# RWKV scan: block inverses from 16- and 32-wide products of non-zero blocks, and a later place for VectorE's second running sum

## The chip, the core and the metric

One core of a Trainium2 chip runs the whole program in one launch. The metric is the device time of one execution in microseconds. The engines are TensorE (PE, with its weight loads as PEld), VectorE (DVE), ScalarE (ACT), GpSimd (POOL) and SyncE (SP), which here only issues DMAs.

## The reference

Two layers of a diffusion transformer at batch 1, 512 tokens of 1024 with a context of 256. Layer 0 mixes by neighbourhood attention and a Hyena convolution, layer 1 by an RWKV-7 scan in both directions; each is followed by a SwiGLU network. The change lies in the scan of layer 1, whose step is

```python
def update(s, w_t, k_t, v_t, kk_t, a_t):
    sa = jnp.einsum('ebhvk,ebhk->ebhv', s, kk_t)
    return s * w_t[..., None, :] - sa[..., :, None] * (kk_t * a_t)[..., None, :] + v_t[..., :, None] * k_t[..., None, :]
```

over 256 + 512 tokens, 16 heads of 64, directions e = 0 and e = 1 (the second reversed), with a readout of the 512.

## The kernel before, in words

The scan is done in chunks of 64 tokens, 12 chunks per head and direction. Within a chunk the steps couple through a strictly triangular 64x64 matrix A, so the kernel needs the inverse of (1 + A) for 12 chunks x 2 directions x 2 heads. A tile of 128 partitions holds two heads' channels; the scan walks over the eight such tiles (`CT` = 8). Chunks are laid out as (p, j): p = 0, 1 is the half of the partitions, j = 0 to 5; h is the head.

The loop `ROUNDS` (line 2031) is a software pipeline written out by hand: in one round, tile i is solved and scanned, tile n = i + 1 is prepared (decays, Gram matrices), tile c = i + 2 has its keys normalised. Every engine has its own copy of the loop, `scan_pe` (2193), `scan_act` (2539), `scan_dve` (2667), `scan_pool` (2153) and `scan_sp` (2057). `Marks` (1968) numbers the finished operations of each engine, and waits are on these numbers, so the tables `PEM`, `DV`, `AC` and `PO` (1985 to 2005) are the order of work. TensorE's products go to PSUM banks in turns, two banks for each name of `BACK` and `FRONT`.

The inverse of tile i is made in this way.

- Masked A (`mask_gram`, `mA_0`, `mA_1`) of tile n comes from the Gram products `A_0`, `A_1` (L2259). SyncE writes its 16x16 diagonal blocks to DRAM with eight DMAs (L2106) and reads them back with one (L2109), one block to a partition of `BLK`.
- GpSimd inverts them in fifteen elimination steps (L2179, L2180: `sub`) and transposes them (`turn`, L2188). SyncE writes both forms to DRAM (L2131), and eight DMAs (L2137) put them on the diagonal of `XY`, which GpSimd has cleared (L2166). `XY` holds for e = 0, 1 the inverse X (a = e) and its transpose Y (a = 2 + e), 64x64 for each (h, j), zero outside the blocks. `xy_in` counts these DMAs.
- In the next round TensorE doubles the blocks twice (`squares`, L2245): 24 products of 64x64 each for `w16_e` = A X, masked by VectorE to the blocks just off the diagonal (`level`, L2688); `x16_e`, `y16_e` = the products of Y and X with it, taken off X and Y (`lessen`, L2692); then `w32_e` and `y32_e` in the same way for blocks of 32. That is 10 x 24 = 240 products and ten VectorE operations of 768 elements per partition.
- The finished Y is the left side of the solves `oo_0`, `oo_1`, `oo_2` (L2307), evicted by ScalarE (L2581). Then come the transition `mr` (L2319), states, outputs and the chain over the chunks (L2385, VectorE L2784).

Between these stand tile n's LoRA product `l01`, `l11` (L2228), tile i-1's transpose `vr` (L2418), and on VectorE tile n's running sums of the log decay (`sums`, L2698, one for each direction), `kin` (L2704), `ba` (L2709), `bt` (L2713), which `A_0` and `A_1` need.

Of the kernel before, what the change touches and what calls it, by code (L numbers as in the profile page):

```python
# [40 lines left out]
def shape_constants():  # L41
# [33 lines left out]
    lev = []  # L75
    for m in (16, 32):
        same = (s // (2 * m)) == (q // (2 * m))
        later = same & (s % (2 * m) >= m) & (q % (2 * m) < m)
        lev.append([later, later.T])
    lev = np.array(lev).astype(f4)  # L80
    t["levelmask"] = np.ascontiguousarray(np.tile(lev.transpose(2, 0, 1, 3), (2, 1, 1, 1)))
# [7 lines left out]
def hybrid_dit_kernel(nc, a, out):  # L89
# [3 lines left out]
    with ctx:  # L93
# [1775 lines left out]
        def mixes_dve(v):  # L1869
# [44 lines left out]
        TOKK, KINT, BVT, XY, OO, MT, NE = carve(ARENA[3], [2 * T, 2 * T, 2 * T, 4 * T, 4 * T, 2 * T, 2 * T])  # L1914
        KROOT, VROOT, KA1, W2S, A2S, BLK, YB, PROD, XB, LV, RSTEP, G2S, G2S2 = carve(
            ARENA[5], [2 * NCH // 2, L // TC, CT, 128, 128, 512, 512, 512, 512, 4 * TC, 2 * L, 128, 128])
# [8 lines left out]
        WI = OO[:, 0:2 * T]  # L1925
        OO = OO.rearrange("p (e h j o t) -> p e h j o t", e=2, h=2, j=6, o=2)
        KM, WI, KINT, BVT = (x.rearrange("p (e h j t) -> p e h j t", e=2, h=2, j=6) for x in (KM, WI, KINT, BVT))
# [7 lines left out]
        LV = LV.rearrange("p (l d t) -> p l d t", l=2, d=2)  # L1935
# [32 lines left out]
        class Marks(dict):  # L1968
# [36 lines left out]
        PO = Marks(pool_done, ((1, "s00 s10 s01 s11 sub turn"),))  # L2005
# [10 lines left out]
        BACK = "w16_0 w16_1 x16_0 y16_0 x16_1 y16_1 w32_0 w32_1 y32_0 y32_1 oo_0 oo_1 oo_2 mr_0 mr_1 mr_2 n_0 yt n_1".split()  # L2016
# [136 lines left out]
        def scan_pool(pool):  # L2153
            sub = Chain(pool, sub_step)
            for _, n, _ in ROUNDS:
# [975 lines left out]
```

## Time and profile before

| | us |
|---|---|
| median of 3 runs | 2502.8 |
| lowest, highest | 2498.32, 2507.42 |
| profiled execution, its own time | 2497.23 |
| its span | 2495.4 |
| TensorE, VectorE, ScalarE, GpSimd busy | 2289.3, 947.5, 655.8, 863.6 |

The span runs from the first to the last instruction on the engines; the execution's time adds what lies around it. In the timeline a group of like instructions is one row, with the time from the first start to the last end, the number of records, and in brackets how long the engine was idle before it and what ended that ("issue": it waited for nothing that the profile shows). An f32 matmul of the program makes two matmul records and two weight-load records on TensorE; an order listing, below, counts it once. The scan's eight rounds with a tile i run from 1541 to 2022 us.

### The profile page before, as it was taken

What the parts mean: (1) busy time and instruction counts of PE and PEld (TensorE: products, weight loads), DVE (VectorE), ACT (ScalarE), POOL (GpSimd) and SP (SyncE); (2) the same over time, 40 slices, a digit from 0 to 9 for tenths busy, and PEclk for the clock granted to TensorE, in tenths of its full rate; (3) what the DMA queues carried; (4) which work ended last, traced back from release to release, by engine and by line L of the source; (5) the groups of instructions that cost most, each with busy time, mean ns of one, the idle gap of its engine ahead of it and who ended that gap; (6) DMA issues with size and microseconds to landing.
All of it is one profiled execution on the core that took longest, in us unless ns stands there. A gap on an engine that the chain in (4) does not pass through costs nothing. (4 is left out here: it accounts for less than half of the span.)

```text
span 2495.4 us, 50322 instructions
## 1 busy us (share of the span) xinstructions
PE 2289.3 (92%) x22240; PEld 1919.4 (77%) x22240; DVE 947.5 (38%) x1499; ACT 655.8 (26%) x1019; POOL 863.6 (35%) x699
## 2 busy tenths in 40 slices
PE   5999989979699999999969998999999987999997
PEld 3778855655399999999828987888888765888785
DVE  3112265980410000122397125676777524000123
ACT  4111066421410000122232133444444223011112
POOL 2222300100133434434215453333333243666562
PEclk9999999989799999999979999999999988999998
DMA  6555530001012121111212342222222121222221
GB/s 255 207 210 187 211 111 18 1 34 42 26 60 67 59 65 61 59 67 60 53 59 67 108 158 56 43 42 43 43 43 41 23 96 66 92 92 93 92 94 66
DMA packets 139265, 204.05 MB, mean 82 GB/s; under 512 B 87783, under 2 KB 97511, under 8 KB 131912
## 3 DMA queue, kind: packets, MB, share of 16 engines
q1 hardware_dynamic: 139080, 201.26, 25.0%
q8 instruction: 155, 2.54, 0.4%
q14 instruction: 30, 0.25, 0.0%
HBM read 183.93 MB, written 17.30 MB: 81 GB/s over the span
## 5 line engine op out<-in xcount | busy, mean ns | idle before, releaser
L258 POOL CAST TMP_r<-WR 128x1024 fp32r<-128x1024 f32 x120 | 126.8, 1056 | 728.2 <-DMA WR<-in_ffn_w_dram 438.4
L277 PE MATMUL PS<-H_r,TMP_r 128*128 128x384 f32 (+1 forms) x1088 | 330.2, 359 | 10.9 <-DVE Y_r L494 10.9
L277 PE MATMUL PS<-Y_r,TMP_r 128*128 128x384 f32 (+1 forms) x1088 | 330.0, 358 | 3.7 <-DVE H_r L494 3.7
L260 POOL TENSOR_TENSOR WR_r<-WR,TMP_r 128x1024 fp32r<-128x1024 f32 x120 | 289.5, 2412 | 9.6
L417 DVE TENSOR_TENSOR P<-TMP,PS 128x768 f32 (+1 forms) x44 | 36.1, 821 | 562.9 <-PE PS L277 562.9
L277 PEld LDWEIGHTS PS<-H_r,TMP_r 128*128 128x128 f32 x1088 | 202.2, 190 | 27.4 <-DVE Y_r L494 11.6
L277 PEld LDWEIGHTS PS<-Y_r,TMP_r 128*128 128x128 f32 x1088 | 201.5, 190 | 19.3 <-DVE H_r L494 4.0
L277 PE MATMUL PS<-H_r,WR_r 128*128 128x384 f32 x736 | 191.4, 341 | 0.0
L400 ACT ACTIVATE TMP<-PS 128x768 f32<-128x768 f32 (+1 forms) x44 | 31.0, 706 | 526.5 <-PE PS L277 526.5
L594 PE MATMUL PS<-H_r,TMP_r 128*128 128x384 f32 x704 | 150.8, 336 | 3.2 <-DVE H_r L632 2.2
L277 PE MATMUL PS<-Y_r,WR_r 128*128 128x512 f32 x352 | 139.4, 396 | 0.0
L277 PEld LDWEIGHTS PS<-H_r,WR_r 128*128 128x128 f32 x736 | 133.4, 189 | 0.0
L594 PEld LDWEIGHTS PS<-H_r,TMP_r 128*128 128x128 f32 x704 | 124.5, 188 | 3.8 <-DVE P L417 2.5
L1750 PE MATMUL PS<-P_r,TMP_r 128*128 128x384 f32 (+1 forms) x448 | 114.4, 348 | 5.9 <-POOL WR_r L2149 4.3
L594 PE MATMUL PS<-Y_r,TMP_r 128*128 128x512 f32 x352 | 109.7, 393 | 2.2 <-DVE Y_r L632 2.2
L270 POOL TENSOR_TENSOR WR_r<-WR,TMP_r 128x1024 fp32r<-128x1024 f32 x44 | 107.2, 2437 | 3.5
L1633 PE MATMUL PS<-H_r,TMP_r 128*128 128x384 f32 x352 | 94.7, 351 | 7.6 <-POOL WR_r L260 7.4
L268 POOL CAST TMP_r<-WR 128x1024 fp32r<-128x1024 f32 x44 | 46.7, 1061 | 153.7 <-DMA WR<-in_down_dram 153.7
L2147 POOL CAST TMP_r<-WR 128x1024 fp32r<-128x1024 f32 x24 | 42.6, 1776 | 144.2 <-DMA WR<-in_rw_w_rkv_dram 144.2
L1633 PE MATMUL PS<-H_r,WR_r 128*128 128x384 f32 x352 | 92.3, 344 | 0.0
L632 DVE TENSOR_TENSOR H_r<-P,H_r 128x768 fp32r<-128x768 f32 x44 | 44.2, 1042 | 124.2 <-ACT H_r L625 124.2
L1750 PE MATMUL PS<-P_r,WR_r 128*128 128x384 f32 (+1 forms) x320 | 91.3, 350 | 0.0
(320 smaller groups left out, 4538.3 us busy)
## 6 DMA issues: line engine op xcount, KB each, us to landing
WR<-in_ffn_w_dram SPq DMA_DIRECT2D x88, 512.0 KB, 3.5
TMP<-in_mod_w_dram SPq DMA_DIRECT2D x40, 1024.0 KB, 4.9
WR<-in_down_dram SPq DMA_DIRECT2D x44, 512.0 KB, 3.5
WR<-in_mix_w_in_dram SPq DMA_DIRECT2D x24, 512.0 KB, 7.0
WR<-in_rw_w_rkv_dram SPq DMA_DIRECT2D x24, 512.0 KB, 4.2
P<-in_mod_w_dram SPq DMA_DIRECT2D x4, 2048.0 KB, 21.7
vkr_dram<-extra SPq DMA_DIRECT2D x16, 384.0 KB, 4.8
scan_front<-vkr_dram SPq DMA_DIRECT2D x16, 384.0 KB, 4.0
```

The costliest lines, as they stand in the source:

```text
L258: nc.gpsimd.tensor_copy(hi, raw).then_inc(weights_hi, 1)
L260: nc.gpsimd.tensor_tensor(lo, raw, hi.bitcast(F32), ALU.subtract).then_inc(weights_split, 1)
L268: nc.gpsimd.tensor_copy(hi, raw).then_inc(weights_hi, 1)
L270: nc.gpsimd.tensor_tensor(lo, raw, hi.bitcast(F32), ALU.subtract).then_inc(weights_split, 1)
L277: last = nc.tensor.matmul(PS[:, bank + b, 0:h1 - h0], w, x[:, h0:h1], start=k + p == 0, stop=k == CT - 1 and p == 2)
L400: nc.scalar.activation(as_halves(GATE[:, u, 0:d.n], d.n), halves(bank, d.n), ACT.Silu)\
L417: nc.vector.tensor_tensor(as_halves(dst, d.n), as_halves(GATE[:, u, 0:d.n], d.n), halves(4 * u + 2, d.n), ALU.mult).then_inc(d.unit_free, 1)
L594: last = nc.tensor.matmul(PS[:, bank, 0:h1 - h0], w[:, at:at + 128], x[:, q % 4, h0:h1], start=k + p == 0, stop=k == FT - 1 and p == 2)
L632: nc.vector.tensor_tensor(d.lo[:, q % 4, :], P[:, q % FT, 0:d.n], d.hi[:, q % 4, :].bitcast(F32), ALU.subtract).then_inc(hid_split, 1)
L1633: last = nc.tensor.matmul(PS[:, 2 * u + b, 0:HALF], w, x[:, HALF * b:HALF * b + HALF], start=k + p == 0, stop=k == CT - 1 and p == 2)
L1750: last = nc.tensor.matmul(PS[:, kept_bank(t) + b, 0:h1 - h0], wt, x[:, k, h0:h1], start=k + p == 0, stop=k == CT - 1 and p == 2)
L2147: nc.gpsimd.tensor_copy(hi, raw).then_inc(weights_hi, 1)
```

## The change

The two levels of doubling no longer multiply whole 64x64 matrices.

- `XY` holds pairs of 16-blocks, 32 columns instead of 64 (the DMAs put block b at column 16 (b mod 2)); it has half its size. `W16`, `W32` and `YF` are new tiles, `WI` and the level masks go, and a table `EDGE` of four columns takes the masks' place.
- First level: `w16` is 96 products (32 rows, 32 columns of A, 16 moving columns), on four row quarters in turn. One VectorE operation masks both directions into `W16`. `xy16` is 2 x 96 such products into two banks, and two VectorE operations take them off X and Y.
- Second level: `w32` is 48 products of 32x32, which VectorE negates into `W32`; `y32` is 96, half with `W32`, half with the identity, which brings the later block beside the earlier; VectorE copies one half of each direction's answer to `YF` (`yf_0`, `yf_1`).
- The other part of `YF`, the diagonal blocks, is made by GpSimd from `XY` (`yd_0`, `yd_1`, after `y16`), ahead of clearing `XY`; the clearing now waits for `y32` and not for `oo_2`.
- The solves read `YF`. `oo_0` and `oo_1` follow each other, and `oo_2` stands before `A_1`.
- On VectorE `sums(n, 1)` moves from between the answers of the first level to behind them and `f1`.

Per round this makes 96 + 192 + 48 + 96 = 432 products in place of 240.

On TensorE, one round from its first level to the transition, in the order of before (`TMP` and `scan_small` are the LoRA operands; `x48` counts matmuls of the program):

```order
L2245 MATMUL PS<-scan_back,scan_tokens 64x64 x48
L2245 MATMUL PS<-scan_back 64x64 x48
L2228 MATMUL PS<-TMP,scan_small 128x384 x4
L2245 MATMUL PS<-scan_back 64x64 x48
L2418 MATMUL PS<-ident,extra 128x128 x4
L2245 MATMUL PS<-scan_back,scan_tokens 64x64 x48
L2245 MATMUL PS<-scan_back 64x64 x48
L2307 MATMUL PS<-scan_back 64x128 x16
L2259 MATMUL PS<-scan_tokens,scan_front 64x64 x24
```

The same stretch after the change, where lines 2448 and 2450 alternate 96 times in all:

```order
L2408 MATMUL PS<-scan_back,scan_tokens 32x16 x96
L2246 MATMUL PS<-TMP,scan_small 128x384 x4
L2421 MATMUL PS<-scan_small,scan_back 32x16 x96
L2421 MATMUL PS<-scan_back,scan_small 32x16 x96
L2467 MATMUL PS<-ident,extra 128x128 x4
L2434 MATMUL PS<-scan_back,scan_tokens 32x32 x48
L2448 MATMUL PS<-scan_back,scan_small 32x32
L2450 MATMUL PS<-scan_back,scan_front 32x32
```

Behind it follow L2316 (`oo_0`, `oo_1`) x32, one Gram x24, L2316 (`oo_2`) x16 and the other Gram. Every inverse product has moved from the 64x64 form to 32-wide forms, and there are more of them.

On VectorE, the same round before, from the first level's answer to the second's (L2698 is the running sum, L2803 `f1`):

```order
L2688 TENSOR_TENSOR scan_back<-PS,scan_small 128x768 x2
L2698 SCALAR_TENSOR_TENSOR scan_front<-extra,scan_front 128x768
L2692 TENSOR_TENSOR scan_back<-scan_back,PS 128x768 x2
L2698 SCALAR_TENSOR_TENSOR scan_front<-extra,scan_front 128x768
L2692 TENSOR_TENSOR scan_back<-scan_back,PS 128x768 x2
L2803 SCALAR_TENSOR_TENSOR extra<-extra,PC,PS 128x512
```

and after the change:

```order
L2732 TENSOR_TENSOR scan_small<-PS,scan_small 128x2x12x16
L2759 SCALAR_TENSOR_TENSOR scan_front<-extra,scan_front 128x768
L2737 TENSOR_TENSOR scan_back<-scan_back,PS 128x2x12x16 x2
L2857 SCALAR_TENSOR_TENSOR extra<-extra,PC,PS 128x512
L2759 SCALAR_TENSOR_TENSOR scan_front<-extra,scan_front 128x768
L2748 TENSOR_SCALAR scan_small<-PS 128x384
L2765 TENSOR_TENSOR scan_tokens<-scan_front 128x12x63
```

The second running sum now stands behind both answers and `f1`, and before the second level's answer (L2748).

The diff, cut to its core:

```diff
-        TOKK, KINT, BVT, XY, OO, MT, NE = carve(ARENA[3], [2 * T, 2 * T, 2 * T, 4 * T, 4 * T, 2 * T, 2 * T])
+        TOKK, KINT, BVT, XY, YF, OO, MT, NE = carve(ARENA[3], [2 * T, 2 * T, 2 * T, 2 * T, 2 * T, 4 * T, 2 * T, 2 * T])
...
-            (0, "w16_0 w16_1 x16_0 y16_0"), (1, "l01 l11"), (0, "x16_1 y16_1"), (-1, "vr"),
-            (0, "w32_0 w32_1 y32_0 y32_1 oo_0"), (1, "A_0"), (0, "oo_1"), (1, "A_1"),
-            (0, "oo_2 mr_0 mr_1"), (1, "kT_0"), (0, "mr_2 n_0 cg yt"), (1, "kT_1"), (0, "n_1"), (1, "tV"),
+            (0, "w16"), (1, "l01 l11"), (0, "xy16"), (-1, "vr"),
+            (0, "w32 y32 oo_0 oo_1"), (1, "A_0"), (0, "oo_2"), (1, "A_1"),
+            (0, "mr_0 mr_1"), (1, "kT_0"), (0, "mr_2 n_0 cg yt"), (1, "kT_1"), (0, "n_1"), (1, "tV"),
...
-        PO = Marks(pool_done, ((1, "s00 s10 s01 s11 sub turn"),))
+        PO = Marks(pool_done, ((1, "s00 s10 s01 s11"), (0, "yd_0 yd_1"), (1, "sub turn")))
...
-                            sp.dma_start(XY[at:at + BK, :, :, :, BK * b:BK * b + BK].rearrange("s a h j t -> s (a h j) t"),
+                            col0 = BK * (b % 2)
+                            sp.dma_start(XY[at:at + BK, :, :, :, col0:col0 + BK].rearrange("s a h j t -> s (a h j) t"),
...
                 if n:
-                    pool.wait_ge(pe_done, PEM["oo_2", n - 1])
+                    pool.wait_ge(dve_done, DV["y16", n - 1])
+                    for e in range(2):
+                        PO.done(nc.gpsimd.tensor_scalar(YF[:, e, :, :, 32 * e:32 * e + 32], XY[:, 2 + e], EDGE[:, 2 + e:3 + e],
+                                                        None, ALU.mult), f"yd_{e}", n - 1)
+                    pool.wait_ge(pe_done, PEM["y32", n - 1])
+                    pool.wait_ge(pool_done, PO["yd_1", n - 1])
                     sub.link(nc.gpsimd.memset(XY[:, :, :, :, :].rearrange("p a h j t -> p (a h j t)"), 0.0))
...
+            def first_level(i):
+                b = back("w16", i)
+                pe.wait_ge(xy_in, 128 * i + 128)
...
+                out = sixteen(b)
+                for e in range(2):
+                    for h, j in ALL_HJ:
+                        for g, r in enumerate(Q4):
+                            c = 32 * (g % 2)
+                            last = nc.tensor.matmul(out[r, e, h, j, :], AM[r, i % 2, e, h, j, c:c + 32],
+                                                    XY[r, e, h, j, EARLIER[e]], start=True, stop=True)
+                PEM.done(last, "w16", i)
+
+            def first_inverse(i):
...
+                    out = sixteen(bank)
+                    for e in range(2):
+                        for h, j in ALL_HJ:
+                            for r in Q4:
+                                last = nc.tensor.matmul(out[r, e, h, j, :], left(r, e, h, j), right(r, e, h, j),
+                                                        start=True, stop=True)
+                PEM.done(last, "xy16", i)
+
+            def second_level(i):
...
+                            last = nc.tensor.matmul(out[late, h, j, :], AM[early, i % 2, e, h, j, c:c + 32],
+                                                    XY[early, e, h, j, :], start=True, stop=True)
+                PEM.done(last, "w32", i)
+
+            def second_inverse(i):
...
+                            nc.tensor.matmul(out[early, h, j, :], W32[late, h, j, :], XY[late, 2 + e, h, j, :],
+                                             start=True, stop=True)
+                            last = nc.tensor.matmul(out[late, h, j, :], IDENT2[late, c:c + 32], XY[late, 2 + e, h, j, :],
+                                                    start=True, stop=True)
+                PEM.done(last, "y32", i)
...
                 if here(i):
-                    lessen(i, "x16_0", XY[:, 0])
-                    lessen(i, "y16_0", XY[:, 2])
-                if here(n):
-                    sums(n, 1)
-                if here(i):
-                    lessen(i, "x16_1", XY[:, 1])
-                    lessen(i, "y16_1", XY[:, 3])
+                    first_inverse(i)
...
                 if here(n):
+                    sums(n, 1)
+                if here(i):
+                    second_level(i)
+                if here(n):
                     after("kmul", n)
                     keys(n, 0)
                 if here(i):
-                    level(i, 1, 0)
-                    level(i, 1, 1)
+                    second_inverse(i, 0)
+                    second_inverse(i, 1)
                 if here(n):
                     based(n, 0)
```

## Rows read from the trace of the kernel before

**Rows 1.** The page: span, and the DMA queue (kind: packets, MB, share).

```profile
span 2495.4 us, 50322 instructions
...
q8 instruction: 155, 2.54, 0.4%
```

**Rows 2.** Windows (us; each engine: busy, records; PEclk, DMA share, GB/s), one round.

```profile
1848.70:1908.90 60.20, 57.48 (x1584) 49.62 (x1584) 44.39 (x73) 27.66 (x40) 21.62 (x38) 1.00 0.22 44
```

**Rows 3.** Timeline of TensorE (start, us, line, xcount, idle before), three rounds.

```profile
1726.50 4.47 PE L2245 MATMUL PS<-scan_back,scan_tokens 64*64 64x64 f32 x96 [2.24 <-DMA scan_back<-inv_dram]
1730.70 3.17 PE L2245 MATMUL PS<-scan_back 64*64 64x64 f32 x96
...
1848.70 3.01 PE L2245 MATMUL PS<-scan_back,scan_tokens 64*64 64x64 f32 x96 [0.45 <-DMA scan_back<-inv_dram]
1851.52 2.99 PE L2245 MATMUL PS<-scan_back 64*64 64x64 f32 x96
...
1865.42 1.80 PE L2307 MATMUL PS<-scan_back 64*64 64x128 f32 x29
...
1869.72 0.93 PE L2259 MATMUL PS<-scan_tokens,scan_front 64*64 64x64 f32 x48
...
1968.45 3.02 PE L2245 MATMUL PS<-scan_back,scan_tokens 64*64 64x64 f32 x96 [0.95 <-DMA scan_back<-inv_dram]
...
1983.23 5.29 PE L2307 MATMUL PS<-scan_back 64*64 64x128 f32 x93
```

**Rows 4.** Timeline of SyncE's queue and GpSimd, 1811 to 1848.

```profile
1811.27 4.43 SPq L2106 DMA_DIRECT2D blk_dram<-scan_tokens  x8
...
1840.03 5.81 SPq L2137 DMA_DIRECT2D scan_back<-inv_dram  x8
...
1819.80 0.23 POOL L2179 TENSOR_TENSOR scan_small<-scan_small 96x30 f32<-96x30 f32 x1 [4.32 <-DMA scan_small<-blk_dram]
```

**Rows 5.** Timeline of weight loads with "issue", and windows between them.

```profile
1938.00 0.13 PEld L2342 LDWEIGHTS PS<-scan_tokens,scan_back 64*64 64x64 f32 x2 [0.49 <-issue]
...
1945.94 0.21 PEld L2345 LDWEIGHTS PS<-scan_back,scan_tokens 64*64 64x64 f32 x8 [0.16 <-issue]
...
1957.60 0.21 PEld L2286 LDWEIGHTS PS<-scan_tokens,scan_front 64*64 64x64 f32 x8 [0.26 <-issue]
...
1937.99:1945.91 7.92, 7.91 (x254) 5.48 (x255) 5.35 (x8) 2.03 (x4) 4.53 (x10) 1.00 0.15 39
1945.92:1957.58 11.66, 10.52 (x255) 8.86 (x254) 8.52 (x25) 4.06 (x5) 9.77 (x21) 1.00 0.05 15
```

**Rows 6.** Timeline of TensorE and windows around the longest such stall.

```profile
1998.72 0.30 PE L2342 MATMUL PS<-scan_tokens,scan_back 64*64 64x64 f32 x8
...
1999.19 0.30 PE L2342 MATMUL PS<-scan_tokens,scan_back 64*64 64x64 f32 x8
...
2000.45 0.28 PE L2345 MATMUL PS<-scan_back,scan_tokens 64*64 64x64 f32 x4 [0.93 <-issue]
...
1998.10:1998.20 0.10, 0.10 (x21) 0.10 (x17) 0.00 (x0) 0.00 (x0) 0.00 (x0) 1.00 0.68 164
...
2001.60:2001.70 0.10, 0.00 (x0) 0.00 (x0) 0.10 (x1) 0.10 (x1) 0.00 (x0) 1.00 0.84 164
```

**Rows 7.** Timeline of VectorE and GpSimd: operations of 768, 512 elements, running sum.

```profile
1858.29 1.79 DVE L2692 TENSOR_TENSOR scan_back<-scan_back,PS 128x768 f32<-128x768 f32 x2
...
1710.63 0.68 DVE L2749 TENSOR_TENSOR scan_tokens<-PS,extra 128x512 f32<-128x512 f32 x1
...
1856.62 1.75 DVE L2698 TENSOR_TENSOR_SCAN scan_front<-extra,scan_front 128x768 f32<-128x768 f32 x1
...
1727.77 1.63 POOL L2161 TENSOR_SCALAR scan_front<-scan_front 128x768 f32<-128x768 f32 x2 [14.55 <-ACT scan_front L2543]
```

**Rows 8.** Windows with the granted clock: first level of a round, chain of the last.

```profile
1728.00:1731.00 3.00, 3.00 (x62) 3.00 (x61) 0.96 (x1) 0.47 (x1) 1.40 (x2) 0.50 0.00 0
...
2005.00:2006.00 1.00, 0.83 (x12) 0.65 (x13) 0.58 (x3) 0.30 (x1) 0.00 (x0) 0.50 0.00 0
```

More of the change, by code:

```diff
@@ L73, in shape_constants @@
     t["grammask"] = np.tile(gram, (2, 1, 1, 1)).astype(f4)
[L75 to L81, printed above, removed]
+    edges = np.stack([i % 32 >= 16, i % 32 < 16, i % 64 < 32, i % 64 >= 32], 1)
+    t["edges"] = edges.astype(f4)
     run = np.ones((128, T), f4)
@@ L2238, in tokens @@
                 PEM.done(last, name, n)
-            def squares(b, lhs, rhs):
-                for j in range(6):
-                    for h in range(2):
-                        for p, pr in enumerate(H2):
-                            last = nc.tensor.matmul(PS[pr, b + h, 64 * j:64 * j + 64], lhs(pr, h, j), rhs(pr, h, j),
-                                                    start=True, stop=True)
-                return last
             def turned(n, e):
@@ new lines, in first_inverse @@
+            def first_inverse(i):
+                b = back("xy16", i)
+                pe.wait_ge(dve_done, DV["w16", i])
+                for bank, left, right in ((b, lambda r, e, h, j: XY[r, 2 + e, h, j, :], lambda r, e, h, j: W16[r, e, h, j, EARLIER[e]]),
+                                          (b + 1, lambda r, e, h, j: W16[r, e, h, j, :], lambda r, e, h, j: XY[r, 2 + e, h, j, LATER[e]])):
+                    out = sixteen(bank)
+                    for e in range(2):
+                        for h, j in ALL_HJ:
[3 more added lines that the diff above has]
+                PEM.done(last, "xy16", i)
@@ new lines, in second_level @@
+            def second_level(i):
+                b = back("w32", i)
+                pe.wait_ge(dve_done, DV["x16", i])
+                out = thirty_two(b)
+                for h, j in ALL_HJ:
+                    for e in range(2):
+                        for p in range(2):
+                            early, late = Q4[2 * p + e], Q4[2 * p + 1 - e]
+                            c = 32 * (1 - e)
+                            last = nc.tensor.matmul(out[late, h, j, :], AM[early, i % 2, e, h, j, c:c + 32],
+                                                    XY[early, e, h, j, :], start=True, stop=True)
+                PEM.done(last, "w32", i)
@@ new lines, in second_inverse @@
+            def second_inverse(i):
+                b = back("y32", i)
+                pe.wait_ge(dve_done, DV["y16", i])
+                pe.wait_ge(dve_done, DV["w32", i])
+                for e in range(2):
+                    out = thirty_two(b + e)
+                    for h, j in ALL_HJ:
+                        for p in range(2):
+                            early, late = Q4[2 * p + e], Q4[2 * p + 1 - e]
+                            c = 32 * (1 - e)
+                            nc.tensor.matmul(out[early, h, j, :], W32[late, h, j, :], XY[late, 2 + e, h, j, :],
[3 more added lines that the diff above has]
+                PEM.done(last, "y32", i)
@@ L2411, in scan_pe @@
                 if here(i):
-                    level("x16", 1, "w16", Ym, Wm)
-                    level("y16", 1, "w16", Wm, Ym)
+                    first_inverse(i)
                 if here(i - 1):
@@ L2420, in scan_pe @@
                 if here(i):
-                    for e in range(2):
-                        level("w32", e, "x16", Am, Xm)
-                    for e in range(2):
-                        level("y32", e, "w32", Wm, Ym)
-                    pe.wait_ge(dve_done, DV["y32_0", i])
+                    second_level(i)
+                    second_inverse(i)
+                    pe.wait_ge(pool_done, PO["yd_1", i])
+                    pe.wait_ge(dve_done, DV["yf_0", i])
                     pe.wait_ge(act_done, AC["bv_1", i])
                     solve(i, "oo_0", [(0, j) for j in range(4)])
+                    pe.wait_ge(dve_done, DV["yf_1", i])
+                    solve(i, "oo_1", [(1, j) for j in range(4)])
                 if here(n):
@@ L2432, in scan_pe @@
                 if here(i):
-                    pe.wait_ge(dve_done, DV["y32_1", i])
-                    solve(i, "oo_1", [(1, j) for j in range(4)])
+                    solve(i, "oo_2", [(e, j) for e in range(2) for j in (4, 5)])
                 if here(n):
@@ L2441, in scan_pe @@
                 if here(i):
-                    solve(i, "oo_2", [(e, j) for e in range(2) for j in (4, 5)])
                     transition(i, 0)
@@ L2788, in scan_dve @@
                 if here(i):
-                    level(i, 0, 0)
-                    level(i, 0, 1)
+                    first_level(i)
                 if here(n):
```

88 lines of the change are left out of this document (48 added, 40 removed), and 4 rows, old and new, of the table DV.

## The prediction

> **What bounds the kernel now.** The page comes first: the profiled execution spans 2495.4 us [rows 1]. The change touches only the scan, so the next view is busy time by stretch. Seven of the eight iterations of the scan take about 60 us each; in the one I use, 1848.7 to 1908.9, TensorE is busy 57.5 of 60.2 us with 1584 matmul records, and as many weight-load records [rows 2]. Each f32 matmul of the program is two of each, so it costs four records.
>
> The timeline of TensorE then gives the stretch that the change rewrites [rows 3]. The first level starts at 1848.70, the first solve (L2307) at 1865.42: 16.7 us. The second Gram (L2259) starts at 1869.72 and takes 0.93 us, of which the end overlaps what follows, some 0.75 net; so the masked A is due 21.8 us after the start, give or take VectorE's mask, which follows both before and after. In the last iteration the stretch is 1968.45 to 1983.23, 14.8 us [rows 3].
>
> What releases the next first level is not TensorE's own work. It is the loop over memory: the masked A is sent out at 1811.27, comes back, GpSimd starts its fifteen steps at 1819.80, SyncE reads the results into XY from 1840.03 with eight DMAs, and TensorE starts at 1848.70 after 0.45 us of waiting for them [rows 3, 4]. From mask to start that is 37.4 us, and it does not get shorter. In the other iterations shown TensorE waited 2.24 and 0.95 us for the same DMA [rows 3]. So the two loops are nearly level, and **the time from the start of the first level to the second masked A counts one for one**, seven times; the eighth time the stretch up to the first solve counts.
>
> **The limit that decides.** TensorE's program is not at hand; it comes in pieces. The page has a DMA queue "instruction" with 155 transfers, 2.54 MB in all, 16.4 KB each [rows 1]. Three stalls of weight loads that the trace puts down to "issue", at 1938.00, 1945.94 and 1957.60, lie 254 + 255 and 255 + 254 records apart [rows 5]: with the few waits that aren't counted, 256 records, one piece. How long a piece takes is seen at the longest stall. A transfer starts in 1998.1 to 1998.2, TensorE's records stop, and resume at 2000.45 after 0.93 us; the next transfer starts in 2001.6 to 2001.7 [rows 6]. So a piece can be used 2.35 us after its transfer starts, and the next transfer starts 1.15 us after that: **3.5 us per 256 records, 13.7 ns per record, while only one piece is on its way**. Today's small products run two side by side, 96 matmul records in 2.82 us [rows 3], 14.7 ns per record with the loads counted: just slower than the supply, which is therefore unseen. Four side by side run 32 in 0.47 us, 7.3 ns per record [rows 6], which outruns it; such stretches are short now.
>
> **The change, part by part.** Per iteration the products of the two levels go from 240 matmuls of 64x64 to 96 + 192 + 48 + 96 = 432 of 32x16 and 32x32.
> - TensorE's own work. Now 480 pairs of records at 29.4 ns, 14.1 us. Afterwards 864 pairs. No row has 32x32 products. From above, the 14.7 ns of four 64x64 products side by side [rows 6] give 12.7 us; from below, half of it, 6.4 us, since half the columns are loaded. I take the lower, because the streamed columns shrink by as much or more. By itself that is a gain of 7.7 us.
> - Supply. 432 x 4 = 1728 records, and 24 of the LoRA product (four f32 matmuls) and the four transposes (two records each) in between, are 1752, or 6.8 pieces. At the start the rest of one piece and the next one are there; five or six are fetched within the stretch, 17.5 to 20.9 us, and with what runs before the first and after the last of them the first solve starts 20.0 to 22.5 us after the first level. I take the middle, 21.3 us, against 16.7. An iteration has 3168 records and a few waits, twelve pieces and a half, so both cases alternate.
> - VectorE. Ten operations of 768 elements, 1.79 us for two, become six of 384; one of 512 takes 0.68 [rows 7], so I take 0.5. It saves about 6 us per iteration of an engine that isn't the limit. The second running sum (1.75 us) [rows 7] now stands before the second level's answer. It ends before the supply brings the 96 matmuls' successors, so I cost it at nothing; were the supply no limit, the second level would wait for it some 2 us.
> - GpSimd. Two products of 384 elements (0.8 us, by half of the 1.63 that L2161's two of 768 took) [rows 7] wait for y16 and stand ahead of the clearing of XY; the clearing halves. GpSimd then waits for the blocks from memory for 4.32 us [rows 4], which hides both. The eight DMAs into XY have the same pieces and rows: nothing.
> - Order. The third solve moves ahead of the second Gram. Three solves of 1.75 us (the last iteration's three in a row took 5.29 [rows 3]) and two Grams of 0.75 lie between first solve and masked A, 6.75 us instead of 5.05. What TensorE saves behind it only lengthens its wait for XY.
>
> So without the clock the masked A is due at 21.3 + 6.75 = 28.1 us against 21.8: 6.3 us later, seven times, and 6.5 us in the last iteration: 50.6 us.
> - Clock. After a wait of 2.24 us the granted clock was 0.50, that is 1.2 GHz, in 1728 to 1731, 62 matmul records in 3 us instead of 34 per us [rows 3, 8]; and in the last iteration, where short bursts alternate with waits, it stood at 0.50 in 2005 to 2006 [rows 8]. With the supply as limit TensorE works in bursts of about a third of the time. I expect 1.2 GHz there, which the supply hides, and a start of the solves at that clock. One such stretch cost 1.4 us (96 records in 4.20 us instead of 2.82) [rows 3]; I take something under two, 2.5 us, eight times: 20 us.
>
> Sum: 50.6 + 20 = 70.6 us. The profiled execution took 2497.2 us, so 2567.8. It lies 5.6 us under the median of the runs shown, so I write 2570. Ends: five pieces everywhere and no loss of clock give (20.0 + 6.75 - 21.8) x 7 + 5.2 = 40 us, 2537; six pieces and 3.5 us of clock give 10.95 x 7 + 11.2 = 88, 2585.
>
> **Rivals.**
> 1. *Faster: the supply keeps up.* Then the stretch is 1.5 us for w16, 1.5 for the LoRA, 3.0 for the next 192 matmuls, 1.1 to x16, y16, f1 and the running sum 2.8 more, 0.5 for w32, 1.7 for y32, 0.6 to the first yf: 12.7 us. The masked A comes at 19.5, 2.3 us earlier; seven times, with 4 us in the last iteration, 20 us: 2477. It needs pieces that arrive in less than the 1 us that 128 pairs at 7.4 ns run; the break-even lies where five and a half pieces take 13 us, near 9 ns per record. Against it stand the stalls [rows 5, 6]. The Trainium skill (Runtime: NRT & Kernel Launch, section Instruction fetch mechanics) says that crossing a 16 KiB boundary is mostly hidden; by it this case would hold, and the trace's 0.93 us at such a boundary speaks against. Chance 0.10.
> 2. *Supply as the limit, clock kept:* 2497.2 + 50.6 = 2548. For it: a burst of small products may count as steady work. Chance 0.20.
> 3. *The clock stays down up to the second masked A:* the 6.75 us double, 7 x (6.3 + 6.75) + 12 = 103, 2601. Chance 0.08.
> 4. *Small products don't overlap:* they run at today's 29.4 ns whatever their size; 864 x 29.4 = 25.4 us with LoRA, transposes and handovers about 30 before the first solve, 13.3 us more, and 1.7 for the order: 7 x 15.0 + 13.3 = 118, 2616. The 32 in 0.47 us [rows 6] speak against it. The Trainium skill (TensorEngine Tiling, section Instruction Overhead) says that a small matmul costs as much as one of 60 columns, and that no factor should come from a dimension that is already small; by that the own work is an estimate of 12 to 14 us and the supply still decides. Chance 0.05.
>
> That the stretch lies beside something else and nothing shows: 0.02, since both loops contain it.
>
> **How the numbers follow.** The forecast has 0.55, rivals 2, 3 and 4 0.33: all slower, 0.88. Faster 0.10, same 0.02; 0.3%, 7.5 us, is what a measurement of this kernel can tell from no change. The range, 2535 to 2605, takes in both ends of the forecast, rival 2 and rival 3; it leaves out rival 4 and the faster case, and what a lasting low clock with six pieces would add.
>
> **What would show it.** Right: first solve 20 to 22.5 us after the first level; "issue" stalls every 256 records in it; about 24 transfers more in the instruction queue (1536 matmuls x 4 / 256); the period of an iteration near 69 us, mask to start still 37; granted clock 0.50 within the stretch. Wrong: first solve at 13 us (rival 1), or clock 1.00 throughout (rival 2).

## The result, and the profile after

| | before | after |
|---|---|---|
| median, us | 2503.8 | 2597.6 |
| lowest, highest (4 runs each) | 2498.3, 2507.4 | 2596.9, 2599.8 |
| profiled execution, its span | 2495.4 | 2595.0 |

The changed kernel takes 1.0378 times as long, 95% interval 1.0357 to 1.0398: 94 us slower. The forecast was 2570 in a range of 2535 to 2605. The side and the range hold; of the 94 us the forecast had 67. The two profiled executions, from which all rows below come, differ by 99.6 us of span.

The page of the profile after, its first lines and its instruction queue, is the counterpart of [rows 1]:

```profile
span 2595.0 us, 56426 instructions
...
PE 2302.7 (89%) x25312; PEld 1922.7 (74%) x25312; DVE 895.8 (35%) x1467; ACT 656.8 (25%) x1019; POOL 874.1 (34%) x716
...
q8 instruction: 179, 2.93, 0.5%
```

The instruction queue has 179 transfers instead of 155, 24 more, as worked out from the 1536 additional matmuls. VectorE is busy 52 us less, and the kernel is slower all the same.

The TensorE timeline of one round after the change, 1834.85 to 1862.12, shown without the rows in which L2448 and L2450 alternate one by one (start, duration, engine, line, operation, number of records, idle time before and its cause), is the counterpart of [rows 3]:

```profile
1834.85 1.06 PE L2408 MATMUL PS<-scan_back,scan_tokens 32*32 32x16 f32 x104
1837.35 1.31 PE L2408 MATMUL PS<-scan_back,scan_tokens 32*32 32x16 f32 x88 [1.44 <-issue]
1839.23 2.93 PE L2246 MATMUL PS<-TMP,scan_small 64*128 64x384 f32 x8 [0.57 <-ACT scan_front L2591]
1842.09 2.32 PE L2421 MATMUL PS<-scan_small,scan_back 32*32 32x16 f32 x159
1846.17 0.66 PE L2421 MATMUL PS<-scan_small,scan_back 32*32 32x16 f32 x33 [1.76 <-issue]
1846.62 1.45 PE L2421 MATMUL PS<-scan_back,scan_small 32*32 32x16 f32 x95
1849.65 1.51 PE L2421 MATMUL PS<-scan_back,scan_small 32*32 32x16 f32 x97 [1.57 <-issue]
1851.09 1.11 PE L2467 MATMUL PS<-ident,extra 128*128 128x128 f32 x4
1852.13 0.63 PE L2434 MATMUL PS<-scan_back,scan_tokens 32*32 32x32 f32 x26
1853.47 1.18 PE L2434 MATMUL PS<-scan_back,scan_tokens 32*32 32x32 f32 x70 [0.70 <-issue]
1855.41 0.23 PE L2448 MATMUL PS<-scan_back,scan_small 32*32 32x32 f32 x1 [0.76 <-DVE scan_small L2748]
...
1857.33 0.21 PE L2448 MATMUL PS<-scan_back,scan_small 32*32 32x32 f32 x1 [0.95 <-issue]
...
1861.08 0.20 PE L2448 MATMUL PS<-scan_back,scan_small 32*32 32x32 f32 x1 [1.90 <-issue]
1862.12 6.53 PE L2316 MATMUL PS<-scan_back 64*64 64x128 f32 x61 [0.72 <-DVE scan_back L2753]
```

Read the rows that end in "issue". Between the resumption at 1846.17 and that at 1849.65 lie 33 + 95 = 128 matmul records, with their weight loads 256: one piece (the 256 instructions that one transfer brings). Between 1837.35 and 1846.17 lie 88 + 8 + 159 = 255, two pieces; at the crossing between these two, inside L2421, no stall shows. In all, six pieces go by between 1837.35 and 1861.08, 23.7 us: **3.96 us per piece, 15.5 ns per record**. Over all eight rounds, each from its first such stall to its last, 39 pieces go by at 3.95 us. TensorE computes for 16.9 of the 27.3 us, at half clock. The first solve, L2316, comes 27.3 us after the first level; in the eight rounds it comes 24.1, 26.0, 24.7, 27.8, 27.3, 27.2, 25.9 and 23.8 us after it, 25.8 in the mean, where it was 16.9 before. In the table of waits over 1530 to 2110 us (what was waited for, total, times, longest) the stalls of the section stand first:

```profile
PE PS L2421 <- issue: 28.7, 18, 2.5
PE PS L2408 <- issue: 11.6, 6, 2.3
PE PS L2450 <- issue: 8.7, 6, 2.0
PE PS L2448 <- issue: 7.7, 6, 1.9
PE PS L2408 <- DMA scan_back<-inv_dram: 7.6, 4, 4.0
PE PS L2434 <- issue: 7.3, 8, 2.2
...
PE PS L2448 <- DVE scan_small L2748: 6.7, 8, 1.2
PE PS L2316 <- issue: 4.2, 6, 0.7
```

The six lines with "issue" sum to 68 us, in lines 2408 to 2450 and 2316. Before, the table of the same section has no "issue" at L2245 or L2307.

The start of the next first level lies 37.3 to 40.0 us behind the end of the second Gram, before 37.4 to 40.0: the loop over memory is what it was. GpSimd now gets its blocks later. Its wait for them, 4.32 us in the one round of [rows 4] and 46.0 us in the eight rounds before, is 137.3 us in the eight rounds after (line, operation, count | busy, mean of one in ns | idle before them):

```profile
L2179 POOL TENSOR_TENSOR scan_small<-scan_small 96x30 f32<-96x30 f32 (+7 forms) x120 | 50.5, 421 | 146.0 <-DMA scan_small<-blk_dram 137.3
```

So the loop over memory behind the second Gram did not become longer; the solves and Grams themselves did (experiments 4 and 5). The round from first level to first level went from 61.05 to 73.90 us in the mean of seven, because the end of the second Gram, and the masked A with it, comes 12.7 us later. The question for the experiments is what makes up the 12.7 us.

### The profile page after: what moved, and what is told of

The parts are those of the page before. It is cut to its first block and busy times, and to the rows that moved or that the text cites. A ratio compares the mean times of both kernels' runs of the same rounds, so it can differ in the third digit from the quotient of the medians.

```text
span 2595.0 us, 56426 instructions
## 1 busy us (share of the span) xinstructions
PE 2302.7 (89%) x25312; PEld 1922.7 (74%) x25312; DVE 895.8 (35%) x1467; ACT 656.8 (25%) x1019; POOL 874.1 (34%) x716
## 5 line engine op out<-in xcount | busy, mean ns | idle before, releaser
L2179 POOL TENSOR_TENSOR scan_small<-scan_small 96x30 f32<-96x30 f32 (+7 forms) x120 | 50.5, 421 | 146.0 <-DMA scan_small<-blk_dram 137.3
```

The costliest lines, as they stand in the source:

```text
L2179: sub.link(nc.gpsimd.tensor_tensor(prod, coef, done, ALU.mult))
```

## The experiments

**Theory A**: TensorE's instructions arrive in pieces of 256, and their arrival sets the pace of the section. **Theory B**: the execution of the small products sets it. Beside them stand the clock, the order of solves and Grams, and VectorE's second running sum.

**1. The same instructions, up to four times the columns** (`a_wide`). The edit, in short; 336 of the 432 small products get it, the 96 of `y32` do not.

```diff
-  matmul(out[r, e, h, j, :], AM[r, i % 2, e, h, j, c:c + 32], XY[r, e, h, j, EARLIER[e]])
+  x = flat XY from the same column on, 64 columns (fewer at the tile's end)
+  matmul(PS[r, b, at:at + 64], AM[r, i % 2, e, h, j, c:c + 32], x)
```

> The changed kernel with the moving operand of 336 of its 432 small products widened to 64 columns (what spills over is written again by the next product). The number of instructions is the same, the streamed columns of these products grow from 16 or 32 to 64. Theory A (TensorE's program arrives in pieces of 256 instructions, 3.5 us each, and that sets the pace): between 20 us slower and equal to the changed kernel (2598 us); if the longer streams keep the clock from falling to 1.2 GHz, up to 60 us faster, 2535 to 2600 in all. Theory B (the small products' own execution sets the pace): at least twice the streaming for 288 of them, 5 us more per round, some 40 us slower, 2640 or more. First solve after the first level: A 22 to 26 us, B 30 us or more.

Measured: 2595.3 us, ratio to before 1.0376 (1.0339 to 1.0413), against 1.0378. The clock did rise. By stretch (us, PE busy, records, granted clock, DMA share, GB/s), first level to first solve, and first solve to the end of the second Gram, here:

```profile
1754.30:1782.10 27.80, 15.54 (x877) 0.93 0.04 9
1782.10:1790.40 8.30, 8.30 (x200) 0.82 0.01 2
```

and in the changed kernel:

```profile
1834.85:1862.12 27.27, 16.90 (x877) 0.55 0.03 8
1862.12:1871.74 9.62, 9.62 (x194) 0.68 0.02 3
```

877 records take 27.8 us at clock 0.93 and 27.3 at 0.55, and in the mean of eight rounds the first solve comes 26.3 us after the first level instead of 25.8. The edit moves two things at once, more columns and a higher clock, which could offset each other; what settles it is the idle time, 70 us of "issue" at the same products, 68 in the changed kernel. The section still waits for its instructions, so theory B falls, and here the low clock costs nothing inside it. The expectation of up to 60 us from the clock did not come true.

**2. The same number of instructions as the change adds, put into the kernel before** (`b_pad`, then `b_block`). The results of the added products are used by nothing. In `b_pad` they stand in every group of the two levels but `y32`.

```diff
+  for r in (slice(0, 32), slice(64, 96)):                # b_pad, before each pair of 64x64 products
+      matmul(PS[r, b + h, 384:400], lhs(r, h, j)[:, 0:32], rhs(r, h, j)[:, 0:16])
...
+  for k in range(24):                                    # b_block, ahead of w16_0 and of w32_0
+      for r in four row quarters:
+          matmul(PS[r, bank, 384:400], lhs(...)[:, 0:32], rhs(...)[:, 0:16])
```

> The kernel before with 192 tiny products (32 rows, 32 x 16) added per round, among the 64 x 64 products of the two levels, their results unused: as many TensorE instructions per round as the changed kernel has (768 more, three pieces). Theory A (supply): the first level to the first solve goes from 16.7 to 22 to 26 us, as in the changed kernel, the clock stays at or falls to 1.2 GHz there, 7 to 11 us per round, 55 to 90 us slower than before: 2560 to 2595. Theory B (own execution): 384 pairs at 8.4 ns, 3.2 us per round, 26 us: 2530. Instruction transfers 155 + 24 = 179, stalls with nothing to wait for every 256 records.

Measured: 2891.0 us, 388 slower, four times more than any theory allowed. The rows show another cost, at the first products of a round:

```profile
1868.92 0.24 PE L2246 MATMUL PS<-scan_back,scan_tokens 32*32 32x16 f32 x4 [0.35 <-DMA scan_back<-inv_dram]
1869.08 0.33 PE L2249 MATMUL PS<-scan_back,scan_tokens 64*64 64x64 f32 x4
1869.35 0.24 PE L2246 MATMUL PS<-scan_back,scan_tokens 32*32 32x16 f32 x4
1869.51 0.33 PE L2249 MATMUL PS<-scan_back,scan_tokens 64*64 64x64 f32 x4
```

and later, where the clock has fallen:

```profile
1879.69 0.48 PE L2249 MATMUL PS<-scan_back,scan_tokens 64*64 64x64 f32 x4
1880.10 0.29 PE L2246 MATMUL PS<-scan_back,scan_tokens 32*32 32x16 f32 x4
1880.32 0.48 PE L2249 MATMUL PS<-scan_back,scan_tokens 64*64 64x64 f32 x4
```

Four tiny and four large records take 0.43 us at full clock, where the large alone take 4 x 29.4 ns = 0.12 [rows 3]; at half clock 0.63. The tiny ones cannot be 0.31 us by their own work: in the changed kernel 104 of them take 1.06 us. Each time that tiles of 32 rows and tiles of 64 follow each other, the later ones start 0.16 to 0.27 us after the earlier at full clock, 0.22 to 0.41 at half. 96 such cycles are 41 to 60 us per round, where the large ones alone took 11: 30 to 49 more, and each round grew by 48, most of it at half clock (0.56 in the mean of the stretch). The page has 179 transfers, but no stall "issue" stands at these products: they are slower than the supply. So this kernel said nothing on A and B, and `b_block` puts the tiny products together.

> The kernel before with the same 192 tiny products added per round, but in two solid blocks of 96 (one ahead of the first level, one ahead of the third group of products), four neighbours on the four row quarters, so that the shape of the tiles changes four times per round and not some 190 times as in b_pad. Theory A (supply of instructions): first level to first solve 16.9 + 9 = 26 us as in the changed kernel, 65 to 80 us slower than before, 2568 to 2583. Theory B (own execution): 384 pairs at 8.4 ns and four changes of shape at some 0.16 us, 3.9 us per round, 31 us, 2534. If the changes of shape made b_pad slow (theory C), the 388 us of b_pad are gone but for one of these two sums; if they didn't, b_block is near 2890 too.

Measured: 2573.8 us, ratio 1.0295 (1.0269 to 1.0321), 74 us slower; the number of transfers is 179, as in the changed kernel. The profiled execution was the slowest of the four (2592.5 us, the others 2565.6 to 2574.1), so its rounds lost more than the median's 74 us. From the first added product to the first solve it is 28.3 us in the mean of its eight rounds, 11.4 more than before. From the timeline of one round, 28.8 us long:

```profile
1832.11 0.97 PE L2405 MATMUL PS<-scan_back,scan_tokens 32*32 32x16 f32 x94 [0.49 <-DMA scan_back<-inv_dram]
1835.40 1.56 PE L2405 MATMUL PS<-scan_back,scan_tokens 32*32 32x16 f32 x98 [2.32 <-issue]
1836.89 1.97 PE L2245 MATMUL PS<-scan_back,scan_tokens 64*64 64x64 f32 x30
1839.14 3.78 PE L2245 MATMUL PS<-scan_back,scan_tokens 64*64 64x64 f32 x65 [0.29 <-issue]
...
1851.01 1.11 PE L2405 MATMUL PS<-scan_back,scan_tokens 32*32 32x16 f32 x110
1852.58 0.88 PE L2405 MATMUL PS<-scan_back,scan_tokens 32*32 32x16 f32 x82 [0.46 <-issue]
...
1856.32 1.74 PE L2245 MATMUL PS<-scan_back,scan_tokens 64*64 64x64 f32 x50 [1.33 <-issue]
```

The added products would run in about 1 us per 96 records and wait 2.32 us for their instructions; 98 + 30 = 128 records lie between the two stalls. Theory A's sum was 2568 to 2583, theory B's 2534. Three things make up the growth, and A's sum named them as one. The added products are busy for 4.5 us of this round, the four stalls are 4.4 us, and the rest, some 3 us, goes with the clock, 0.82 in this round: the one round that kept it at 1.00 grew by 7.5 us only (to 24.4). So here, where 64x64 products share the section, the low clock is not free; but the stalls, 31 us in eight rounds where the kernel before has none, are what theory B has no place for. With the changes of shape gone, 314 of `b_pad`'s 388 us are gone too (theory C).

**3. Fewer instructions** (`a_noident`). The 48 products with the identity go, VectorE has two operations more, and the other 48 are reordered so that four neighbours use four row quarters. In short:

```diff
-  matmul(out[early, h, j, :], W32[late, h, j, :], XY[late, 2 + e, h, j, :])
-  matmul(out[late, h, j, :], IDENT2[late, c:c + 32], XY[late, 2 + e, h, j, :])
+  matmul(out[early, h, j, :], W32[late, h, j, :], XY[late, 2 + e, h, j, :])
...
+  yl_e:  YF[:, e, :, :, c:c + 32] = XY[:, 2 + e] * EDGE[:, 3 - e:4 - e]
-  yf_e:  YF[:, e, :, :, c:c + 32] = PS
+  yf_e:  YF[:, e, :, :, c:c + 32] += PS * EDGE[:, 2 + e:3 + e]
```

> The changed kernel without the 48 products with the identity in the last step of the inverse (VectorE copies these blocks instead, two operations more and two with one more operand), the other 48 ordered so that four neighbours use four different row quarters. 192 instructions fewer per round, three quarters of a piece. Theory A (supply): 0.75 x 3.5 us = 2.6 us per round, 8 rounds, 21 us faster than the changed kernel; with the second to last step at 26 ns per pair at the low clock now at half of that, up to 35: 2563 to 2577 us. Theory B (own execution at 8.4 ns per pair): 96 pairs, 0.8 us per round, 6 us: 2591. Instruction transfers of the page: 179 less 6.

Measured: 2568.2 us, ratio 1.0270 (1.0237 to 1.0303), 29 us less than the changed kernel, 173 transfers. The first solve comes 23.2 us after the first level instead of 25.8. 192 instructions at 15.5 ns are 3.0 us; 2.6 are seen. Theory B had 6 us in all; with the 12.6 ns that one of these records took at half clock (128 in 1.61 us) the 96 records that went are 1.2 us per round, 10 us. So B does not reach 29 us either way.

**4. The order of solves and Grams** (`a_order`, `a_noident_order`).

```diff
-  w32 y32 oo_0 oo_1 | A_0 | oo_2 | A_1
+  w32 y32 oo_0 | A_0 | oo_1 | A_1 | oo_2
```

> The changed kernel with the solves and Grams in the order of the kernel before (first solve, first Gram, second solve, second Gram, third solve). If the time to the second masked A counts one for one, the third solve (1.75 us at 2.4 GHz, 3.5 at 1.2) leaves the loop in seven rounds: 12 to 20 us faster than the changed kernel, 2578 to 2586 us. If the order is hidden: 2598.

> Both edits of a_noident and a_order together. If both count one for one on the same path, their gains add: 29 + 11 = 40 us less than the changed kernel, 2557 us. If a supply that is the limit makes the order worthless (TensorE gets its instructions no sooner), 2565 to 2570.

Measured: 2586.7 us (1.0335, 1.0303 to 1.0368) for the order alone, 11 less than the changed kernel; 2553.5 us (1.0228, 1.0194 to 1.0261) for both edits, 15 less than the products alone. The 95% intervals of the ratios overlap within each pair, but the single runs do not (2582.6 to 2588.3 against 2596.9 to 2599.8; 2545.4 to 2559.6 against 2565.7 to 2572.2). The gains add, so the order counts one for one, at 11/7 to 15/7, 1.6 to 2.1 us per round; by the traces the second Gram ends 1.6 and 1.7 us earlier. The forecast's step had 1.7.

**5. The clock where the supply no longer hides it** (`a_noident_wide`, `a_all`). `a_noident` with the edit of experiment 1 on all its small products; `a_all` has the order of experiment 4 as well.

> a_noident (2568 us) with the moving operand of nearly all its small products widened to 64 columns, now also of the products just ahead of the solves, so that the granted clock is high when the solves start. In the changed kernel the stretch from the first solve to the end of the second Gram took 9.1 us where 6.75 were due at 2.4 GHz. If the low clock is what those 2.4 us are (theory: clock costs where the supply no longer hides it), they go, eight times: 19 us less, 2549, and the first solve comes as late as before (23.2 us after the first level). If the clock is worth nothing there: 2568. If the wider streams themselves count: more than 2575.

> a_noident_wide with the old order of solves and Grams, all that helped together. If the gains add: 2598 - 29 for the products - 11 to 15 for the order - 19 for the clock = 2535 to 2540, still some 35 us behind the kernel before, which is the supply of 576 instructions more per round at 13.7 to 15.5 ns. To beat before it would have to come below 2497.

Measured: 2558.4 us (1.0249, 1.0226 to 1.0273) and 2552.8 us (1.0218, 1.0196 to 1.0241). The first is 10 us less than `a_noident`, half of the 19 expected, with intervals that overlap; the second is no better than `a_noident_order` and missed its sum, 2535 to 2540, by 13 us. The edit kept the clock up to the solves in three of the seven full rounds. Two of these and two others, each window from the first solve to the first Gram (the 64 records of `oo_0` and `oo_1`, and the first of the Gram's):

```profile
1836.12:1839.60 3.48, 3.48 (x68) 1.00 0.02 5
1904.35:1907.80 3.45, 3.45 (x68) 1.00 0.02 5
1765.74:1771.30 5.56, 5.55 (x68) 0.61 0.01 3
1973.67:1979.30 5.63, 5.63 (x64) 0.59 0.01 3
```

The first two solves take 3.5 us together at clock 1.00 and 5.6 at 0.6: 2.1 us more. From the first solve to the end of the second Gram it is 6.8 to 6.9 us in the three rounds at full clock, close to the forecast's 6.75, and 8.3 to 9.8 in the changed kernel, 9.0 in the mean: 2.2 more. So the price of the clock per round is shown by rows; that taking it away would shorten the whole by 8 x 2.2 us is not shown, since no run kept it up everywhere.

**6. The second running sum alone** (`b_sum` on the kernel before; in `a_sum_early`, on the changed one, it goes back ahead of the answers `x16`, `y16`, directly behind the first sum).

```diff
-  x16_0 y16_0 | scan_1 | x16_1 y16_1 | f1 | kin_0 | w32_0
+  x16_0 y16_0 x16_1 y16_1 | f1 | scan_1 kin_0 | w32_0         # b_sum
```

> The kernel before with only VectorE's second running sum moved, behind the answers x16, y16 and f1, ahead of the first keys. Theory A: VectorE has been idle there behind TensorE, 2496 to 2510, no change. Rival: it now stands ahead of the second level's masks, TensorE waits 1.75 us for w32 in each round, 7 to 14 us slower, 2510 to 2518.

> The changed kernel with VectorE's second running sum back ahead of the answers x16 and y16 (both running sums stand together behind the first answer). The trace has VectorE wait 1.49 us for TensorE at the second level's answer, so the place of the sum is hidden in either case: no change, 2590 to 2605. Rival: it now delays x16, and with it the second level, by up to 1.75 us per round, 8 to 14 us slower.

Measured: `b_sum` 2507.9 us, ratio 1.0036 (1.0021 to 1.0051), 7.6 us slower. That lies inside the first theory's 2496 to 2510 and below the rival's 2510 to 2518, but the interval excludes no change, and the rows show the rival's wait, so the rival's mechanism held at the low end of its size. Its table of waits over the scan has

```profile
PE PS L2245 <- DVE scan_back L2688: 11.6, 7, 1.7
```

where the kernel before has 0.7 us in three waits. In seven rounds TensorE waits 1.7 us for the mask of the second level, behind the sum. `a_sum_early` took 2591.2 us, ratio 1.0364 (1.0341 to 1.0386): within the changed kernel's interval, as expected. So the later place of the sum, the second half of the change, costs 7.6 us by itself and nothing that can be told from no change beside the first half. That the stalls for instructions are what covers it is argued, not shown.

**7. The second level alone, small and without extra instructions** (`b_level2`, `b_level2_order`). 96 products of 32x32 in place of 96 of 64x64, so 240 products per round as before.

```diff
-  w32_0 w32_1 y32_0 y32_1: 24 products of 64x64 each, 4 VectorE operations of 768
+  matmul(PS[late, b, at:at + 32], AM[early, ..., cl:cl + 32], XY[early, e, h, j, ce:ce + 32])       # w32, 48
+  matmul(PS[early, b + e, at:at + 32], WI[late, ...], XY[late, 2 + e, h, j, cl:cl + 32])            # y32, 48
+  WI = -PS;  XY[:, 2 + e, :, :, cl:cl + 32] += PS * (1 on the early rows)
...
-  f1 kin_0 | w32 | ba_0 | y32_0 y32_1 | bt_0                   # b_level2
+  f1 | w32 | kin_0 | y32_0 | ba_0 bt_0 | y32_1                 # b_level2_order
```

> The kernel before with the second level alone in the changed form: 48 + 48 products of 32 x 32 in place of 96 of 64 x 64, no product with the identity, four abreast; VectorE has three operations of 384 elements where it had four of 768. The number of TensorE instructions is that of before. Theory A (instructions set the pace): products of a quarter of the work run no faster than their instructions come, 192 pairs at 2 x 13.7 ns instead of 29.4; what is left is VectorE's handovers, 1 to 3 us per round: 2480 to 2500 us, and the instruction queue has 155 transfers. Theory B (own execution sets the pace): 192 pairs at 8.4 instead of 29.4 ns, 4 us, and the handovers: 5 to 7 us per round, 2450 to 2465.

> b_level2 with VectorE's order fitted to the shorter products: the answer w32 stands ahead of the first keys, y32_0 ahead of the first ba and bt, y32_1 behind them. In b_level2 TensorE waited 1.8 us eight times for w32 (12.8 us in all), behind f1 and the first keys (0.94 us). Theory: some 1.1 us of that and part of the 0.7 us ahead of the first solve go, 8 to 12 us less than b_level2: 2490 to 2495, faster than before by 0.2 to 0.4%; first solve at 15 us instead of 16.2. Rival: the instructions of the section (984 per round, 3.84 pieces of 3.5 to 4 us, 13.5 to 15.2 us) come no faster, and the wait turns into stalls with nothing to wait for: 2500.

Measured: 2503.1 us (1.0012, 0.9997 to 1.0028) and 2499.0 us (0.9997, 0.9983 to 1.0012). Neither can be told from the kernel before; both intervals lie within 0.3% of it. Theory A's 2480 to 2500 was missed by 3 us, theory B's 2450 to 2465 by 38; of `b_level2_order` the forecast, 2490 to 2495, was missed and the rival, 2500, held. In `b_level2` the two steps of the second level take 1.01 and 1.17 us in one round instead of 3.0 each (as the first level's two in [rows 3]), and TensorE waits for VectorE instead. The wait tables of the scan's rounds, `b_level2`:

```profile
PE PS L2424 <- DVE scan_back L2841: 12.8, 8, 1.8
PE PS L2312 <- DVE scan_back L2849: 5.8, 8, 0.7
```

and `b_level2_order`:

```profile
PE PS L2424 <- DVE scan_back L2838: 6.8, 8, 1.0
PE PS L2312 <- DVE scan_back L2847: 5.8, 8, 0.7
...
PE PS L2424 <- issue: 5.3, 5, 1.4
```

6.0 us of waiting for VectorE went, and 5.3 us of "issue" came at the same line. Its first solve stands at 14.3 to 17.2 us and its rounds take 58.7 to 64.1 us, short and long in turns, 61.15 in the mean; before it was 61.05. The kernel before already needs 984 records in 16.9 us, 17.2 ns each, where a piece under stall brings them in 15.5: the section is close to the supply, and a cheaper product has little to gain. No version tried beats the kernel before. Whether fewer instructions than 240 x 4 would was not tried.

## Why the prediction was right, and where its size was off

Per round, in us behind the first level (rows with + are differences):

| step | forecast | measured | by |
|---|---|---|---|
| first solve, before | 16.7 | 17.2 | mean of the seven full rounds |
| first solve, after | 21.3 | 26.1 | the same |
| third solve ahead of the second Gram | +1.7 | 1.6 to 2.1 | experiment 4 |
| solves at low clock | +2.5 | 2.2 | experiment 5 |
| end of the second Gram, before | 21.8 | 22.5 | mean of seven |
| end of the second Gram, after | 30.6 | 35.2 | mean of seven |
| mask to next first level | no change | no change | starts of the rounds |

- *What counts.* The loop over memory set the period as forecast, and each microsecond between first level and second masked A counted in seven rounds: 7 x 12.7 = 89 us, and 9.0 in the last round up to its first solve (23.8 against 14.8), 98 of the 99.6 us between the two profiled executions.
- *Supply.* The mechanism, the size of a piece and the 24 additional transfers were right. **The term that was mis-sized is "five or six are fetched within the stretch, 17.5 to 20.9 us, and with what runs before the first and after the last of them the first solve starts 20.0 to 22.5 us after the first level": the first solve came 26.1 us after it.** Six are fetched in the round shown, but one takes 3.96 us and not the 3.5 of a single pair of transfers [rows 6], 23.7 us in place of 20.9; and 2.5 us pass before the first and 1.0 behind the last. I took the spacing of one stall for that of a long row of them, and left too little for the two ends. The forecast's own sign, first solve 20 to 22.5 us after the first level, did not hold: it came at 23.8 to 27.8. The second Gram came 4.6 us later than forecast; 0.7 of that was in the mean of the kernel before as well (22.5 against the 21.8 of the round I used). 7 x 3.9 = 27 us, which is what the forecast lacks.
- *Why a piece took longer.* The prediction read from [rows 6] that the next transfer starts 1.15 us after TensorE resumes. At 31 of the 43 stalls inside the eight sections it does so (1.05 to 1.19 us after at thirty of them, 1.63 at one); at the other twelve it starts 2.2 to 2.5 us after. In exactly these twelve the first product of a new group, at which TensorE checks another engine's progress (a handover), stands within 37 matmul records of the resumption; at the others it is 44 or more away. Of the 31 pieces with a stall at both ends, 25 took 3.3 to 4.0 us, and the six behind such a late start 4.7 to 5.3. Windows (us, PE busy, records, granted clock, DMA share, GB/s) behind the resumption at 1774.32, late, and behind that at 1849.65:

```profile
1774.32:1776.60 2.28, 2.28 (x85) 0.50 0.00 0
1776.70:1776.80 0.10, 0.10 (x26) 0.50 0.87 164
1849.65:1850.70 1.05, 1.05 (x80) 0.50 0.00 0
1850.70:1850.80 0.10, 0.10 (x23) 0.50 0.82 164
```

  That the handovers cause the late starts is read from the trace; no run varied it.
- *The number.* The measured 2597.6 us lies above the forecast's own upper end, 2585. It is inside the range because the range took in rival 3 (2601), whose mechanism did not happen: the stretch from the first solve to the end of the second Gram took 9.0 us, not 13.5. That the range held is in that part luck. The prediction also counted an iteration after the change as 3168 records; that is the count of before, and with 768 more it is 3936, 15.4 pieces. Its conclusion that the two cases alternate stands: five or six stalls lie inside each section.
- *Own work.* 104 matmul records of 16 columns took 1.06 us at full clock, 10 ns each, inside the bounds of 7.4 to 14.7; at half clock 12.6 to 15 ns. The 7.4 taken was too low, and the 12 to 14 us of rival 4's estimate too high: 864 x 10 ns is 8.8 us. It didn't matter, since the supply decides.
- *Clock.* The section ran at a granted clock of 0.55 in the mean of the round shown, mostly the lower level, 1.2 GHz, and experiment 1 shows that this is free there. What solves and Grams lose is 2.2 us against 2.5. Rival 2 needed a high clock, which no round had (0.50 to 0.63).
- *VectorE and GpSimd.* Costed at nothing, and `a_sum_early` shows no cost of the sum's place. The reason given, that the sum ends before the supply brings the next products, just holds: in the round shown it ends at 1854.66, and the products whose answer VectorE then copies from 1854.70 end at 1854.65. In the kernel before the later place costs 7.6 us (`b_sum`). The handovers are not free, though: TensorE waits 6.7 us in eight rounds for the copy of the second level's answer, L2748.
- *Rival 1* (supply keeps up) is refuted by 68 us of stalls. The Trainium skill (Runtime: NRT & Kernel Launch, section Instruction fetch mechanics) says that a crossing of a 16 KiB boundary is mostly hidden; this trace does not agree for such a section, since a crossing inside it stalls TensorE for up to 2.5 us. *Rival 4* (no overlap) is refuted by the 10 ns.

## What to carry to other kernels

Count a dense stretch in instructions as well as in columns: here a piece of 256 took 3.3 to 5.3 us to come, 3.95 in the mean, and work that asked for more than one record in 15 ns waited for its instructions. An f32 matmul of this kernel is four records however small it is, so cutting a product into many smaller ones multiplies the records, which are scarce here, and shrinks the work, which is not. Before splitting, divide the time of the present stretch by its records; at the 17 ns per record of this kernel smaller products won nothing.

## What the runs showed of the hardware that was not expected

- Tiles of 32 rows and tiles of 64 rows that alternated on TensorE (`b_pad`) hardly overlapped. A cycle of four records each took 0.43 us at full and 0.63 us at half clock, against some 0.16 at full clock by the rates that each kind has in a row of its own (4 x 29.4 and 4 x 10 ns): 0.14 us per change of shape, and 388 us over the kernel for 192 products of 16 columns per round, against 74 us for the same number in solid blocks. The Trainium skill (TensorEngine Tiling, section Key Properties) says that a change of tiling mode drains the engine. The trace agrees so far as the later products start 0.16 to 0.27 us after the earlier ones at full clock; the drain itself shows in no row.
- The pace of instructions did not follow TensorE's clock: 877 records took 27.8 us at 0.93 and 27.3 at 0.55.
- The transfer of the next piece started later where a handover stood soon after TensorE's resumption: 2.2 to 2.5 us behind it instead of 1.05 to 1.19, at 12 of 43 stalls.
- More streaming raised the granted clock and not the speed. With 64 instead of 16 or 32 columns in 336 products of a round, the rounds' sections ran at 0.76 to 0.95 where they had been granted 0.50 to 0.63.
